# Final norm of all rows beside the last two experts of a mixture-of-experts layer, their own rows normed by index behind it

## What is computed

```python
def _rmsnorm(x, g):
    xf = x.astype(jnp.float32)
    y = xf * lax.rsqrt(jnp.mean(xf * xf, axis=-1, keepdims=True) + EPS)
...
    gate, idx = lax.top_k(jnp.swapaxes(aff, 1, 2), cap)
    xs = h[bidx, idx]
    a = jnp.einsum('becd,edf->becf', xs, w_e_gate)
    u = jnp.einsum('becd,edf->becf', xs, w_e_up)
    y = jnp.einsum('becf,efd->becd', jax.nn.silu(a) * u, w_e_down)
    y = y * gate[..., None].astype(h.dtype)
    return jnp.zeros_like(h).at[bidx, idx].add(y)
...
    x = x + gt2 * _ec_moe(h, ...)
y_prompt, y_sample = _rmsnorm(xp, norm_final_g), _rmsnorm(xs, norm_final_g)
```

## Time and profile before

| what | us |
|---|---|
| median of 3 runs | 2811.98 (2808.2 to 2813.47) |
| the profiled execution, its own time | 2812.37 |
| its span in the trace | 2810.7 |
| PE busy in the span | 2520.6 (90%) |
| DVE busy in the span | 1616.4 (58%) |
| ACT busy in the span | 1179.4 (42%) |
| POOL busy in the span | 422.9 (15%) |

### The profile page before, as it was taken

How to read it: one execution, slowest core, us unless ns; L and a number is a source line. 1 busy time by engine, 2 the same in 40 slices (tenths; PEclk the granted TensorE clock), 3 DMA queues, 4 the chain that set the end, 5 groups by cost and what they waited for, 6 DMA issues and landing times.

```text
span 2810.7 us, 42821 instructions
## 1 busy us (share of the span) xinstructions
PE 2520.6 (90%) x16163; PEld 2242.1 (80%) x16163; DVE 1616.4 (58%) x2964; ACT 1179.4 (42%) x1928; POOL 422.9 (15%) x467
## 2 busy tenths in 40 slices
PE   5579999999996799898279999999999999999990
PEld 2568878687875577676079999999999999999990
DVE  1576949497794533432745555555555555556543
ACT  3546453554422323332134444444444444444443
POOL 1020110101000210110022202112220211222100
PEclk9889999999997789888589999999999999999995
DMA  5885565656537342413146556666655656665537
GB/s 202 296 290 194 166 235 188 236 190 215 180 137 240 110 136 92 157 72 112 44 154 184 166 169 196 183 184 197 184 163 171 196 183 183 196 185 162 171 107 293
DMA packets 297629, 500.23 MB, mean 178 GB/s; under 512 B 14142, under 2 KB 251291, under 8 KB 281658
## 3 DMA queue, kind: packets, MB, share of 16 engines
q1 hardware_dynamic: 275258, 376.96, 40.1%
q0 software_dynamic: 22272, 121.94, 14.7%
HBM read 401.98 MB, written 96.88 MB: 177 GB/s over the span
## 4 chain that ended last, share of the span: by engine, by line
PE 81%; DVE 5%; DMA 2%; ACT 2%; issue 1%; POOL 1%; POOLq 0%; SPq 0%; DVEq 0%; ACTq 0%
PE bank L1196 23%; PE bank L1197 22%; PE bank L1198 22%; PE bank L1314 2%; PE bank L1376 2%; PE bank L1570 1%; PE bank L1578 1%; DVE work_out L1835 1%; PE bank L1442 1%; PE bank L1407 1%; PE bank L1341 1%; PE bank L1353 1%; DVE work_exp L2028 1%; PE bank L1433 1%; DMA work_exp<-x_rows 1%
## 5 line engine op out<-in xcount | busy, mean ns | idle before, releaser
L1196 PE MATMUL bank<-act_hl_exp,hl_exp 128*128 128x288 f32 x3072 | 917.5, 299 | 0.0
L1197 PE MATMUL bank<-act_hl_exp,hl_exp 128*128 128x288 f32 x3072 | 907.1, 295 | 0.0
L1198 PE MATMUL bank<-act_hl_exp,hl_exp 128*128 128x288 f32 x3072 | 904.2, 294 | 0.0
L1198 PEld LDWEIGHTS bank<-act_hl_exp,hl_exp 128*128 128x128 f32 x3072 | 579.2, 189 | 0.0
L1197 PEld LDWEIGHTS bank<-act_hl_exp,hl_exp 128*128 128x128 f32 x3072 | 577.6, 188 | 0.0
L1196 PEld LDWEIGHTS bank<-act_hl_exp,hl_exp 128*128 128x128 f32 x3072 | 576.6, 188 | 0.4
L2120 DVE TENSOR_TENSOR hl_exp<-work_exp,hl_exp 128x1024 fp32r<-128x1024 f32 x192 | 233.9, 1225 | 268.7 <-ACT hl_exp L924 268.7
L2120 DVE TENSOR_TENSOR hl_exp<-raw_exp,hl_exp 128x1024 fp32r<-128x1024 f32 x192 | 233.5, 1224 | 214.1 <-ACT hl_exp L924 214.1
L1788 DVE SCALAR_TENSOR_TENSOR work_proj<-work_proj,wcv 128x392 f32<-128x392 f32 (+11 forms) x600 | 343.2, 641 | 0.0
L924 ACT ACTIVATE hl_exp<-work_exp 128x1024 fp32r<-128x1024 f32 x192 | 202.9, 1057 | 253.6 <-PE bank L1198 253.6
L924 ACT ACTIVATE hl_exp<-raw_exp 128x1024 fp32r<-128x1024 f32 x192 | 200.5, 1053 | 156.4 <-PE bank L1198 152.7
(11 more groups left out here) (281 smaller groups left out, 3661.6 us busy)
## 6 DMA issues: line engine op xcount, KB each, us to landing
hl_proj<-park_w POOLq DMA_DIRECT2D x80, 1024.0 KB, 5.5
raw_exp<-in_w_e_gate_dram SPq DMA_DIRECT2D x32, 1024.0 KB, 5.2
raw_exp<-in_w_e_up_dram SPq DMA_DIRECT2D x32, 1024.0 KB, 5.2
work_exp<-in_w_e_gate_dram SPq DMA_DIRECT2D x32, 1024.0 KB, 5.2
work_exp<-in_w_e_up_dram SPq DMA_DIRECT2D x32, 1024.0 KB, 7.9
raw_exp<-in_w_e_down_dram SPq DMA_DIRECT2D x32, 1024.0 KB, 5.9
work_exp<-in_w_e_down_dram SPq DMA_DIRECT2D x32, 1024.0 KB, 5.2
park_w<-hl_proj SPq DMA_DIRECT2D x10, 2048.0 KB, 13.5
```

Source lines behind the costliest of these rows:

```text
L1196: pe.matmul(out, lh, rh, start=first, stop=False)
L1197: pe.matmul(out, lh, rl, start=False, stop=False)
L1198: return pe.matmul(out, ll, rh, start=False, stop=last_)
```

## The change

The loops over experts end two experts earlier (`NE - 3` in place of `NE - 2`), and experts 14 and 15 are written out. A number u = 0 to 23 counts their units: u = 0 to 11 are the units of expert 14, and 12 to 23 those of expert 15.

- All 18 blocks of `x2_rows` (as they stand after expert 13) go through a ring of six blocks, in six groups of three. SP's `load_rows` puts groups 0 and 1 behind the weight load of u = 7, after a wait for the scatter of expert 13, and groups 2 to 5 behind u = 13, 16, 19 and 22. `store_rows` stores groups 0 to 4 behind u = 11, 14, 17, 20 and 23, and group 5 at the end. ACT's `roots` for group n runs at the end of u = 4 + 3n; DVE's `norm_rows` at the end of u = 5 + 3n. The three roots of a group are one instruction.
- POOL's scatter of expert 14 also waits until all 18 blocks are loaded. When it has landed, POOL gathers the rows of expert 15 (into `last_y`, the freed `xg`) and those of expert 14 (into `fix`) from `x2_rows`. DVE's `out_rows` of expert 15 waits for these gathers (`f_gx`) and adds its product to `last_y`; expert 15 is not scattered.
- ACT's `fix_roots` at the end of u = 21 and DVE's `norm_rows` at u = 22 norm the rows of expert 14. `last_roots` squares 768 columns of the rows of expert 15, then the last 256, and takes the roots; DVE norms the three blocks.
- POOL writes the normed rows of expert 14 and then, when those have landed, of expert 15 into the outputs by index. It starts when all plain stores have landed. The meeting of all engines, the loads behind it and the old loops of ACT and DVE over 18 blocks are gone.

```diff
+        GRP, NGRP = 3, NTILE // 3
         W5 = carve(work5, WORK, [("raw2", 2 * KC * 256), ("xg", 3 * (D + NE)), ("h32", 2 * CAP), ("sg", 2 * CAP),
-                    ("hx", 2 * CAP), ("yT", 4 * CAP), ("y", 3 * D), ("gate", 4)])
+                    ("hx", 2 * CAP), ("yT", 4 * CAP), ("y", 3 * D), ("gate", 4), ("ring", 2 * GRP * D),
+                    ("fix", 3 * D), ("g", D), ("junk", D)])
...
+        ring = W5["ring"].rearrange("p (b d) -> p b d", b=2 * GRP)
+        fix = W5["fix"].rearrange("p (t d) -> p t d", t=3)
+        last_y = xg[:, :, 0:D]
+        NST = NTILE + 6
         stat6 = logits.rearrange("p t e -> p (t e)")
-        W6 = carve(work5, WORK, [("x", NTILE * D), ("g", D), ("junk", 2 * D)])
-        x6 = W6["x"].rearrange("p (b d) -> p b d", b=NTILE)
-        FIN = (0, 2, 6, 12, NTILE)
+        sq6, rt6, rc6, part6 = (stat6[:, NST * i:NST * i + NST] for i in range(4))
+        ROWS = ((0, 128), (1, 128), (2, CAPP))
...
+            with sp.Fori(1, NE - 2) as e:
                 expert_units(e, range(NEXP))
-            stage_end(sp, 3)
-            sp.dma_start(W6["g"], norm_final_g.partition_broadcast(128)).then_inc(f_x[0], 16)
-            for u in range(len(FIN) - 1):
-                sp.dma_start(x6[:, FIN[u]:FIN[u + 1], :], x2_rows[128 * FIN[u]:128 * FIN[u + 1], :]
-                             .rearrange("(b p) d -> p b d", p=128)).then_inc(f_x[u], 16)
-            for t in range(NTILE):
-                sp.wait_ge(f_y, t + 1)
-                dst = y_prompt[0, 128 * t:128 * t + 128, :] if t < TP // 128 else \
-                    y_sample[0, 128 * t - TP:128 * t - TP + 128, :]
-                sp.dma_start(dst, x6[:, t, :]).then_inc(f_st, 16)
-            sp.wait_ge(f_st, 16 * NTILE)
+
+            def load_rows(n):
+                if n == 0:
+                    sp.wait_ge(e_sc, 48 * (NE - 2))
+                    sp.dma_start(W5["g"], norm_final_g.partition_broadcast(128)).then_inc(f_x[0], 16)
+                elif n > 1:
+                    sp.wait_ge(f_st[n % 2], 16 * GRP * (n // 2))
+                for t in range(GRP * n, GRP * n + GRP):
+                    sp.dma_start(ring[:, t % (2 * GRP), :], x2_rows[128 * t:128 * t + 128, :]).then_inc(f_x[n % 2], 16)
...
+            def store_rows(n):
+                for t in range(GRP * n, GRP * n + GRP):
+                    sp.wait_ge(f_y, t + 1)
+                    dst = y_prompt[0, 128 * t:128 * t + 128, :] if t < TP // 128 else \
+                        y_sample[0, 128 * t - TP:128 * t - TP + 128, :]
+                    sp.dma_start(dst, ring[:, t % (2 * GRP), :]).then_inc(f_st[n % 2], 16)
+
+            for u in range(2 * NEXP):
+                expert_units(NE - 2 + u // NEXP, range(u % NEXP, u % NEXP + 1))
+                if u == 7:
+                    load_rows(0)
+                    load_rows(1)
+                if u >= 11 and u % 3 == 2:
+                    store_rows((u - 11) // 3)
+                if u >= 13 and u % 3 == 1:
+                    load_rows((u - 13) // 3 + 2)
+            store_rows(NGRP - 1)
+            for q in range(2):
+                sp.wait_ge(f_st[q], 16 * GRP * NGRP // 2)
...
+            def square(t, n, src, d0, d1, out):
+                if t > 0:
+                    upto(act, f_sq, t)
+                act.activation(W5["junk"][0:n, d0:d1], src[0:n, d0:d1], ACT.Square, accum_out=out).then_inc(f_sq.sem, 1)
+
+            def roots(n):
+                act.wait_ge(f_x[n % 2], 16 * GRP * (n // 2 + 1) + (16 if n % 2 == 0 else 0))
+                for t in range(GRP * n, GRP * n + GRP):
+                    square(t, 128, ring[:, t % (2 * GRP), :], 0, D, sq6[:, t:t + 1])
+                upto(act, f_sq, GRP * n + GRP)
+                act.activation(rt6[:, GRP * n:GRP * n + GRP], sq6[:, GRP * n:GRP * n + GRP], ACT.Sqrt, bias=eps[:, :],
+                               scale=1.0 / D).then_inc(f_rt.sem, GRP)
+
+            def fix_roots():
+                act.wait_ge(f_gx, 96)
+                for i, n in ROWS:
+                    t = NTILE + i
+                    square(t, n, fix[:, i, :], 0, D, sq6[0:n, t:t + 1])
+                for i, n in ROWS:
+                    t = NTILE + i
+                    upto(act, f_sq, t + 1)
+                    act.activation(rt6[0:n, t:t + 1], sq6[0:n, t:t + 1], ACT.Sqrt, bias=eps[0:n, :],
+                                   scale=1.0 / D).then_inc(f_rt.sem, 1)
+
+            def last_roots():
+                act.wait_ge(e_yev, 8 * (NE - 1) + 6)
+                for i, n in ROWS:
+                    t = NTILE + 3 + i
+                    square(t, n, last_y[:, i, :], 0, 768, sq6[0:n, t:t + 1])
+                for i, n in ROWS:
+                    t = NTILE + 3 + i
+                    upto(act, f_sq, t + 1)
+                    act.activation(part6[0:n, i:i + 1], sq6[0:n, t:t + 1], ACT.Identity, bias=eps[0:n, :],
+                                   scale=1.0 / D).then_inc(f_sq.sem, 1)
+                act.wait_ge(e_yev, 8 * NE)
+                for i, n in ROWS:
+                    square(NTILE + 9 + i, n, last_y[:, i, :], 768, D, part6[0:n, 3 + i:4 + i])
+                for i, n in ROWS:
+                    upto(act, f_sq, NTILE + 10 + i)
+                    act.activation(rt6[0:n, NTILE + 3 + i:NTILE + 4 + i], part6[0:n, 3 + i:4 + i], ACT.Sqrt,
+                                   bias=part6[0:n, i:i + 1], scale=1.0 / D).then_inc(f_rt.sem, 1)
+
+            def expert(e, last, u=None):
...
+                    if u is not None and 4 <= u + j < 4 + 3 * NGRP and (u + j) % 3 == 1:
+                        roots((u + j - 4) // 3)
+                    if u is not None and u + j == 21:
+                        fix_roots()
...
+            with act.Fori(0, NE - 3) as i:
                 expert(i + 1, False)
-            expert(NE - 1, True)
-            stage_end(act, 3)
-            for t in range(NTILE):
-                act.wait_ge(f_x[sum(t >= z for z in FIN[1:])], 32 if t < FIN[1] else 16)
-                if t >= 2:
-                    act.wait_ge(f_sq.sem, f_sq.base + t - 1)
-                act.activation(W6["junk"][:, D * (t % 2):D * (t % 2) + D], x6[:, t, :], ACT.Square,
-                               accum_out=stat6[:, t:t + 1]).then_inc(f_sq.sem, 1)
-                act.wait_ge(f_sq.sem, f_sq.base + t + 1)
-                act.activation(stat6[:, NTILE + t:NTILE + t + 1], stat6[:, t:t + 1], ACT.Sqrt, bias=eps[:, :],
-                               scale=1.0 / D).then_inc(f_rt.sem, 1)
+            expert(NE - 2, False, 0)
+            expert(NE - 1, True, NEXP)
+            last_roots()
...
+                if isinstance(e, int) and e == NE - 2:
+                    for q in range(2):
+                        pool.wait_ge(f_x[q], 16 * GRP * NGRP // 2 + (16 if q == 0 else 0))
...
+            expert(NE - 2, False)
+            pool.wait_ge(e_sc, 48 * (NE - 1))
+            pool.wait_ge(e_gate, NE)
+            for e, rows in ((NE - 1, last_y), (NE - 2, fix)):
+                for t, n in ROWS:
+                    pool.indirect_dma_start(rows[0:n, t, :], None, x2_rows[:, :],
+                                            bass.IndirectOffsetOnAxis(ap=ids[0:n, e, t:t + 1], axis=0)).then_inc(f_gx, 16)
+
+            def rows_out(e, t, n, rows):
+                at = ids_y[0:n, e - (NE - 2), t:t + 1] if t < 2 else ids[0:n, e, t:t + 1]
+                dst = y_sample[0] if t < 2 else y_prompt[0]
+                pool.indirect_dma_start(dst, bass.IndirectOffsetOnAxis(ap=at, axis=0), rows[0:n, t, :], None)\
+                    .then_inc(f_wr, 16)
+
+            for q in range(2):
+                pool.wait_ge(f_st[q], 16 * GRP * NGRP // 2)
+            for t, n in ROWS:
+                pool.wait_ge(f_y, NTILE + t + 1)
+                rows_out(NE - 2, t, n, fix)
+            pool.wait_ge(f_wr, 48)
+            for t, n in ROWS:
+                pool.wait_ge(f_y, NTILE + 3 + t + 1)
+                rows_out(NE - 1, t, n, last_y)
+            pool.wait_ge(f_wr, 96)
...
+                    if isinstance(e, int) and e == NE - 1:
+                        dve.wait_ge(f_gx, 96)
+                    else:
+                        wait_pos(dve, e_sc, 48 * e)
                     dve.wait_ge(e_gate, e + 1)
                 for s, n in ((0, 128), (1, 128), (2, CAPP)):
-                    last = dve.tensor_scalar(y_t[0:n, s, 128 * d:128 * d + 128],
-                                             psum[6 + d % 2][0:n, 128 * s:128 * s + 128], gate_t[0:n, s:s + 1], None,
-                                             ALU.mult)
+                    fixed = isinstance(e, int) and e == NE - 1
+                    y = (last_y if fixed else y_t)[0:n, s, 128 * d:128 * d + 128]
+                    p = psum[6 + d % 2][0:n, 128 * s:128 * s + 128]
+                    if fixed:
+                        last = dve.scalar_tensor_tensor(out=y, in0=p, scalar=gate_t[0:n, s:s + 1], in1=y, op0=ALU.mult,
+                                                        op1=ALU.add)
```

(16 more changed lines are left out.)

43 lines of the change are left out of this document (16 added, 27 removed).

## The result

| | before | changed |
|---|---|---|
| median of 4 runs each, us | 2810.93 (2808.2 to 2813.47) | 2783.36 (2778.08 to 2787.89) |
| ratio, with its 95% interval | | 0.9908 (0.9888 to 0.9927) |
| the profiled execution, its own time | 2812.37 | 2787.89 |
| its span | 2810.7 | 2785.7 |

The sign was forecast, the size was not: 27.6 us came of the 47 that were promised, and 2783.4 lies above the 2779 of the range. The profiled execution is 22.5 us above the 2765.4 of the sum.

A forecast was written before the change was run, and what follows sets the result against it. PE was taken to bound the experts, with nothing covering the 72.1 us end. 2812.4 (profiled execution) - 54.3 for the new end + 7.3 for norm work beside the experts = 2765.4 us; range 2756 to 2779.

The forecast's parts named there:

- What bounds the kernel now: Experts 14 and 15: PE bounds, other engines have 33 to 47 us free each; the 72.1 us end is uncovered.
- The new end: From E, the end of PE's last unit, to the program's end: 17.8 us (bounds 16.5 and 21), saving 54.3.
- Cost 0, with nothing in hand: POOL's chain of loads, scatters and gathers before expert 15's out_rows: rows at 2738, wanted at 2738.4, so no cost.
- Rival B: Gathers land 5 us after DVE wants them, as scatters take up to 9.9 us, not 7; 2771 us, chance 0.16.
- What the norm costs beside the experts: Experts 14 and 15: grouped norm work on ACT and DVE makes PE wait 7.3 us in pieces; bounds 0 and 68.
- A, all hidden: Experts 14 and 15: slack larger than reckoned, so the norm work costs PE nothing; 2758 us, chance 0.15.
- C, a switch that also drains: ACT: nine table switches take 1.38 us more each, about half reaching PE; 2771 us, chance 0.04.
- D: PE's clock falls after the wait at u = 16, so 5 us of matmuls take 10, once or twice; 2773, chance 0.07.
- The slower end, E: ACT and DVE bound every unit of experts 14 and 15; all 68 us lie on the path; 2826 us, chance 0.03.
- F: Program's end: SP's last group stores still run at E + 12, so POOL waits for them; 2776 us, chance 0.03.

The follow-up runs named there:

- ring9: The changed kernel with a ring of nine row blocks instead of six, so the last rows load and gather earlier; median 2772.2 us, ratio to before 0.9837.
- spread: ring9 plus a POOL drain behind the gathers, with norm work cut from groups of three to one block a unit; median 2751.08 us, ratio to before 0.9782.

## Why the prediction was off, step by step

**"What bounds the kernel now": right.** All but 24.8 of the 72.1 us at the end went, and PE is the bound in the experts.

**"The new end", E + 17.8: one of the two steps that failed, by a term left out.** Up to the third issue each term came within a third of a us. DVE's last six `out_rows` took 1.64 us (1.74 forecast), a square of 768 columns comes every 0.97 us (0.96), one of 256 every 0.54 (0.57), the blocks every 1.39, the third issue at E + 12.7 (13.0). The landing was 3.0 us, 1.5 less than the 4.5 taken and below the bound of 3.4, the one input outside its bounds (the 2.4 us in that bound are read to the middle of a slice of rows 11 that begins at 2745.0). But nothing stands behind the landing in that sum, except 0.3 us that it does not name: 13.0 and 4.5 make 17.5. The prediction saw the POOL drain of 7.9 us in rows 2, counted it among what goes with the meeting, and did not ask what it was a price for. It goes by the indirect DMAs since the last drain, and the change takes 3 of the 96 (expert 15's scatter) and adds 12 (gathers and writes): 105. The drain moved to the program's end and grew to 8.64. So the tail is 12.7 + 3.0 + 0.2 + 8.6 + 0.3 = 24.8.

**"Cost 0, with nothing in hand", for the gathers: the other step that failed.** The load of group 5 went out at 2709.0 us, 8.3 us behind the 2694.97 of before once the 5.7 at the mark are taken off (8 forecast). From there each term ran over: 9.9 us to land (8.5), 0.8 until POOL went on, 5.1 from the first scatter's issue to the third's (3.8), 8.3 for it to land (7), 0.3 until POOL went on, 7.6 for the gathers' issues (8.0, the one that ran under), 9.4 until the last had landed and DVE went on (6.9). The rows were there 6.7 us later than the 2738 forecast, and 7.5 later than the 2737.2 that the forecast's own terms add up to. The landing times were those of stretches in which the DMA share was 0.37 to 0.61; the change itself raised it to 0.86 and 0.73, and to 1.02 in the 5 us of the gathers. That the fuller DMA engines made the landings longer fits this and is not shown by a run of its own. Rival B had the kind of event, with a chance of 0.16, but not its size: DVE waited 8.3 us and not 5, and the scatters' landing, its reason, gave only 1.3 of it. Behind the landing it had 8.7 us to E; measured are 10.6, with 1.8 of them from the clock.

**"What the norm costs beside the experts", +7.3: right in sum, 6.8 by ring9, and by its mechanism.** By ring9's windows, in pieces: 1.2 us at u = 8 (1.1 forecast, though the two times given for it lie 1.3 apart), 2.7 at u = 9 and 10 (1.8), 1.7 around the seam (0.8), 1.3 at the Silu of expert 15 (2.9), and nothing like it at u = 17 to 22 (0.7). The places are those followed, all but the last; that the sum fits so well is in part luck, since its pieces are off by up to 1.6 us, some up and some down. That the work comes in groups was the reason given, and spread shows it.

**Rivals.** A, all hidden, is false for this kernel and true for spread. C, a switch that also drains, is false. ACT's first switch in expert 14 of the changed kernel:

```profile
2621.01 0.18 ACT L984 ACTIVATION_READ_ACCUMULATOR work_exp<-work_exp 128x1 f32 x1
2621.27 1.28 ACT L991 ACT_TABLE_LOAD   x1
2622.56 0.30 ACT L991 ACTIVATE logits<-logits,eps 128x3 f32<-128x3 f32 x1
```

The load follows the read within 0.08 us and the root follows the load within 0.01. The drain that the Trainium skill (ScalarE: Activation LUTs, What ACT_TABLE_LOAD costs) adds is not in this trace. D happened in a small way, inside B, with the clock at 0.50 after a stop of PE of 7.4 us. The slower end, E, is far away: with all the added work, spread leaves PE without a gap. F is false: SP's last store had landed by 2749.1, before E.

**The part ahead of the experts** added 5.7 us in the profiled execution. No step could have held that, but the range could: the three runs of before lay 5 us apart, and the prediction took that for the noise. Over all runs here the kernel before spreads over 23 us (2798.71 to 2821.59).

## What to carry to other kernels

- A drain of POOL costs by the number of indirect DMAs since its last one; put it into an idle wait of POOL that is longer than the drain, and when a drain disappears from a place, look for the one that inherits its count.
- When a change fills idle bandwidth, the landing times of the quiet profile can be too short (6.9 us forecast for the last gather, 9.4 here): take those of its busiest stretch, and give a chain with nothing in hand a cost.
- Work that fits by its sum still costs by its burst: one piece per unit instead of three every third unit took 6.9 us off PE's path and left the amount of work alone.
